# The first modulation on TensorE: weights stationary and columns out, half of the scales moved from VectorE and GpSimd

## The reference, cut to what matters

```python
c_act = jax.nn.silu(c)
cc_act = jax.nn.silu(c_ctx)
mod = (c_act @ ada_w[l] + ada_b[l])[:, None, :]
sh1, sc1, g1, sh2, sc2, g2 = jnp.split(mod, N_MOD, axis=-1)
h = modulate(x, sh1, sc1)          # h * (1.0 + scale) + shift
mod_c = cc_act @ ada_w[l] + ada_b[l]
csh1, csc1, ... = jnp.split(mod_c, N_MOD, axis=-1)
hc = modulate(x_ctx, csh1, csc1)
z = h @ w_in                       # the projections of layer 0
```

## Time and profile before

| | us |
|---|---|
| Median of 3 runs | 1854.79 |
| Lowest and highest | 1854.58, 1856.01 |
| Profiled execution | 1850.3 |
| Its span | 1848.4 |
| TensorE busy | 1786.0 (97%) |
| VectorE busy | 1272.5 (69%) |
| ScalarE busy | 891.5 (48%) |
| GpSimd busy | 1001.9 (54%) |

### The profile page before, as it was taken

How to read it: one execution, slowest core, us unless ns; L and a number is a source line. 1 busy time by engine, 2 the same in 40 slices (tenths; PEclk the granted TensorE clock), 3 DMA queues, 4 the chain that set the end, 5 groups by cost and what they waited for, 6 DMA issues and landing times.

```text
span 1848.4 us, 30888 instructions
## 1 busy us (share of the span) xinstructions
PE 1786.0 (97%) x10814; PEld 1535.7 (83%) x10814; DVE 1272.5 (69%) x2158; ACT 891.5 (48%) x1507; POOL 1001.9 (54%) x431
## 2 busy tenths in 40 slices
PE   5999899998999999999999999999999999999999
PEld 1847579997978887788878799999999988888887
DVE  6586667888548777424433369988999957777776
ACT  3033754445445454433353546665555554555553
POOL 4034146443775543775437778877776654444443
PEclk8999999999999999999999999999999999999999
DMA  8787247886665555543325455544544455555554
GB/s 324 260 302 252 87 145 239 281 278 214 209 204 182 182 193 165 178 159 114 103 92 171 159 173 182 182 163 163 166 160 149 149 184 193 193 192 194 193 193 169
DMA packets 95322, 346.00 MB, mean 187 GB/s; under 512 B 10544, under 2 KB 12032, under 8 KB 94592
## 3 DMA queue, kind: packets, MB, share of 16 engines
q1 hardware_dynamic: 78048, 283.67, 46.1%
q10 hardware_dynamic: 17184, 61.11, 9.5%
HBM read 343.66 MB, written 1.08 MB: 187 GB/s over the span
## 4 chain that ended last, share of the span: by engine, by line
PE 74%; DVE 12%; issue 6%; DMA 3%; POOL 3%; ACT 2%; DVEq 0%; ACTq 0%; POOLq 0%; SPq 0%
PE ps L626 26%; PE ps L561 19%; PE ps L573 6%; PE ps L579 3%; POOL ring_lo L506 3%; PE ps L696 2%; PE ps L782 2%; PE ps L545 2%; PE ps L849 2%; DMA ring<-stream 2%; PE ps L796 2%; PE ps L1014 1%; DVE arena L2812 1%; DVE ps L2809 1%; DMA cst<-consts 1%
## 5 line engine op out<-in xcount | busy, mean ns | idle before, releaser
L506 POOL TENSOR_TENSOR ring_lo<-ring,ring_hi 128x1024 fp32r<-128x1024 f32 x371 | 901.6, 2436 | 659.2 <-ACT ring_hi L500 657.6
L500 ACT ACTIVATE ring_hi<-ring 128x1024 fp32r<-128x1024 f32 x502 | 531.9, 1060 | 515.5 <-DMA ring<-stream 513.7
L561 PE MATMUL ps<-h_span,ring_hi 128*128 128x256 f32 x3168 | 416.2, 284 | 0.0
L561 PEld LDWEIGHTS ps<-h_span,ring_hi 128*128 128x128 f32 x3168 | 396.8, 192 | 5.5 <-issue 3.3
L626 PE MATMUL ps<-ring_hi,e_pair 128*128 128x512 f32 x1024 | 253.7, 389 | 0.8 <-DVE e_pair L2840 0.8
L2840 DVE TENSOR_TENSOR e_pair<-arena,e_pair 128x256 fp32r<-128x256 f32 x128 | 174.6, 1364 | 98.9 <-ACT e_pair L1850 98.2
L626 PEld LDWEIGHTS ps<-ring_hi,e_pair 128*128 128x128 f32 x1024 | 192.1, 188 | 41.0 <-issue 1.2
L561 PE MATMUL ps<-h_span,ring_lo 128*128 128x256 f32 x1584 | 222.4, 283 | 0.3 <-POOL ring_lo L506 0.2
L561 PEld LDWEIGHTS ps<-h_span,ring_lo 128*128 128x128 f32 x1584 | 204.3, 192 | 0.9 <-POOL ring_lo L506 0.9
L506 DVE TENSOR_TENSOR ring_lo<-ring,ring_hi 128x1024 fp32r<-128x1024 f32 x141 | 175.2, 1244 | 40.1 <-ACT ring_hi L500 39.9
L626 PE MATMUL ps<-ring_hi,arena_r 128*128 128x512 f32 x672 | 174.5, 392 | 2.2 <-ACT ring_hi L500 2.2
(11 more groups left out here) (301 smaller groups left out, 2305.4 us busy)
## 6 DMA issues: line engine op xcount, KB each, us to landing
ring<-stream SPq DMA_DIRECT2D x540, 512.0 KB, 3.3
arena<-aside_w ACTq DMA_DIRECT2D x49, 512.0 KB, 4.6
late<-aside_w ACTq DMA_DIRECT2D x21, 512.0 KB, 4.6
resid<-aside_w ACTq DMA_DIRECT2D x10, 512.0 KB, 5.8
arena<-scale_w ACTq DMA_DIRECT2D x8, 512.0 KB, 15.9
arena<-ln_rows ACTq DMA_DIRECT2D x8, 512.0 KB, 5.1
arena<-gate_cols ACTq DMA_DIRECT2D x2, 1024.0 KB, 4.9
arena<-decay ACTq DMA_DIRECT2D x1, 1536.0 KB, 6.8
```

Of the source, the lines that this page charges most:

```text
L500: act.activation(ring_hi[:, s, :], ring[:, s, :], ACT.Copy).then_inc(hi_ready, 1)
L506: eng.tensor_tensor(ring_lo[:, s, :], ring[:, s, :], ring_hi[:, s, :], ALU.subtract).then_inc(lo_ready[s], 1)
L561: m = pe.matmul(ps[:, bank, 0:T], w[:, kc * P:(kc + 1) * P], x[:, kc, :], start=begin, stop=w is w_lo and kc == KC - 1)
```

## The change

TensorE now makes twelve blocks: units 0 to 7 are the shifts and 8 to 11 the scale blocks 0 to 3. The weights are stationary, each unit in eight chunks of 128 x 128, and the two columns of `cact` are moving, so that the result comes out as columns in the bank (6, 7, then 3) and needs no copy and no turning. VectorE makes the scale blocks 4 to 7 as before; GpSimd and ScalarE make none. Chunks 4 to 7 of `sc1p` are released when shifts and VectorE's scales are there, chunks 0 to 3 after the third bank. Every chunk of `hcat` gives a semaphore step of its own, and the first projection takes them one by one, in the order 4, 5, 6, 7, 0, 1, 2, 3; the other front projections use the same order. The wait for the identity and the bias row stand after the first projection unit. ScalarE issues `x`, identity and small inputs before its activations of `c_all`, and the constants and `ctx` right after, before it waits for any result.

```diff
-EARLY_ADA = 8
-ASIDE = 2 * ADA_UNITS - 2 * EARLY_ADA
-SCALE_DVE = (0, 1, 2, 3, 4)
-SCALE_POOL = (5, 6, 7)
+EARLY_ADA = 12
+ASIDE = 2 * ADA_UNITS - 16
+SCALE_DVE = (4, 5, 6, 7)
...
-EARLY_BANKS = (4, 5)
+EARLY_BANKS = (6, 7, 3)
+FRONT_ORDER = (4, 5, 6, 7, 0, 1, 2, 3)
...
+            def k_tile(u, rhs, bank, at=0, done=True, first=False):
...
+                for kc in FRONT_ORDER:
+                    if first:
+                        pe.wait_ge(h_dve if kc < 4 else h_act, kc % 4 + 1)
...
-            def early_rows(g):
+            def early_tiles(g):
...
-                for k4 in range(4):
-                    w = unit(FIRST_UNIT["ada0"] + 4 * g + k4)
-                    for k2 in range(2):
-                        kc = 2 * k4 + k2
-                        m = pe.matmul(ps[0:2, b, :], cact[:, kc, :], w[:, k2 * 512:(k2 + 1) * 512],
+                for q in range(4):
+                    w = unit(FIRST_UNIT["ada0"] + 4 * g + q)
+                    for kc in range(KC):
+                        m = pe.matmul(ps[:, b, 2 * q:2 * q + 2], w[:, kc * P:(kc + 1) * P], cact[:, kc, :],
                                       start=kc == 0, stop=kc == KC - 1)
...
             for g in range(EARLY_ADA // 4):
-                early_rows(g)
-                if g == 0:
-                    pe.wait_ge(ident_in, 16)
-                else:
-                    early_columns(g - 1)
-            early_columns(EARLY_ADA // 4 - 1)
-            pe.wait_ge(inputs, 16 * 4)
-            bias_row()
+                early_tiles(g)
...
+                           done=tile_done(n) is not None, first=n == 0)
+                    if n == 0:
+                        pe.wait_ge(ident_in, 16)
+                        pe.wait_ge(inputs, 16 * 4)
+                        bias_row()
...
-            pe.wait_ge(h_dve, 1)
-            pe.wait_ge(h_act, 1)
             projections()
...
+            act.dma_start(h[:, :, :], x_t).then_inc(x_in, 16)
+            act.dma_start(cst[:, 0:P], consts[:, 0:P]).then_inc(ident_in, 16)
+            for dst, src in ((relb[0:32, :], rel_bias), (oneh[0:32, :], onehot), (dmask[0:8, :], dist_mask), (lamb, lam_in)):
+                act.dma_start(dst, src).then_inc(inputs, 16)
             for c, dst in enumerate((c_all, cc_all)):
                 act.wait_ge(c_in[c], 16)
                 act.activation(dst, dst, ACT.Silu).then_inc(c_all_ready, 1)
...
+            act.dma_start(cst[:, P:], consts[:, P:]).then_inc(consts_in, 16)
+            act.dma_start(z, ctx_t).then_inc(ctx_in, 16)
...
+            scale_column(0)
+            scale_column(1)
+            mod_columns(0, EARLY_BANKS[0], 0)
+            scale_column(2)
+            scale_column(3)
             settle()
+            step(dve.tensor_tensor(mod[0][:, SC1 + 4:SC1 + 8, :], mod[0][:, SC1 + 4:SC1 + 8, :],
+                                   param("ada_b0", SC1 + 4, 4).unsqueeze(2).broadcast_to([P, 4, 2]), ALU.add))
+            mod_columns(0, EARLY_BANKS[1], 4)
             settle()
+            for b in EARLY_BANKS[:2]:
+                dve.wait_ge(emptied[b], reads[b].now())
+            scales(4).then_inc(mod_cols, 1)
+            mod_columns(0, EARLY_BANKS[2], 8)
+            dve.wait_ge(emptied[EARLY_BANKS[2]], reads[EARLY_BANKS[2]].now())
+            step(scales(0))
+            settle()
```

More of the change, by code:

```diff
@@ L418, in build @@
         c_in = [sem(f"c_in{c}") for c in range(2)]
-        scale_w_in = [sem(f"scale_w_in{k}") for k in range(8)]
-        scale_product = sem("scale_product")
-        scale_sum = sem("scale_sum")
+        scale_w_in = [sem(f"scale_w_in{n}") for n in range(len(SCALE_DVE))]
         ident_in = sem("ident_in")
@@ L535, in wait_unit_lo @@
                 pe.wait_ge(lo_ready[u % RING], at_trip(i, TRIP // RING, SPLIT_IN_SLOT[u]))
-            def k_tile(u, rhs, bank, i=None, at=0, done=True):
-                w = unit(u, i)
+            def k_tile(u, rhs, bank, at=0, done=True, first=False):
+                w = unit(u)
                 if at == 0:
                     start_fill(bank)
-                for kc in range(KC):
+                for kc in FRONT_ORDER:
+                    if first:
+                        pe.wait_ge(h_dve if kc < 4 else h_act, kc % 4 + 1)
                     r = rhs(kc)
                     n = r.shape[-1]
-                    m = pe.matmul(ps[:, bank, at:at + n], w[:, kc * P:(kc + 1) * P], r, start=kc == 0, stop=kc == KC - 1)
-                    if kc == 0:
+                    m = pe.matmul(ps[:, bank, at:at + n], w[:, kc * P:(kc + 1) * P], r, start=kc == FRONT_ORDER[0],
+                                  stop=kc == FRONT_ORDER[-1])
+                    if kc == FRONT_ORDER[0]:
                         m.then_inc(units_begun, 1)
@@ L1340, in _ @@
                 act.dma_start(dst, all_rows(c_rows, c)).then_inc(c_in[c], 16)
-            for k in SCALE_LOADS[:5]:
-                scale_load(k)
+            for n in range(len(SCALE_DVE)):
+                act.dma_start(scale_in[:, n, :], scale_w[n]).then_inc(scale_w_in[n], 16)
             act.wait_ge(params_in, 16)
@@ L1365, in drain @@
                 act.activation(dst, ps[:, b, 0:n], func, **kw).then_inc(emptied[b], 1)
[L1367 to L1376, removed]
             n_var = Count()
@@ L1391, in _ @@
                 for kc in range(4, KC):
-                    m = act.activation(hcat[:, kc, (1 - c) * T:(2 - c) * T], src[:, kc, :], ACT.Identity,
-                                       scale=sc1p[:, kc, c:c + 1], bias=mod[0][:, SH1 + kc, c:c + 1])
-                m.then_inc(h_act, 1)
+                    act.activation(hcat[:, kc, (1 - c) * T:(2 - c) * T], src[:, kc, :], ACT.Identity,
+                                   scale=sc1p[:, kc, c:c + 1], bias=mod[0][:, SH1 + kc, c:c + 1]).then_inc(h_act, 1)
             def on_all(rows, k):
@@ L2881, in _ @@
             pool.wait_ge(c_all_ready, 2)
[L2882 to L2885, removed]
             for k in range(PAIRED):
@@ L3083, in _units @@
     return [
-        wide(a["ada_w"][0])[:EARLY_ADA], proj,
+        tiles(a["ada_w"][0])[:EARLY_ADA], proj,
         rows(np.concatenate([wo[:512], wo_b]))[list(MIX_ORDER)], *mlp(a["mlp_w1"][0], a["mlp_w2"][0]),
@@ L3099, in _aside @@
     columns = [w.T.reshape(ADA_UNITS, P, D) for w in a["ada_w"]]
-    return (np.ascontiguousarray(columns[0][SC1:SC1 + 8]),
+    return (np.ascontiguousarray(columns[0][[SC1 + k for k in SCALE_DVE]]),
             np.ascontiguousarray(np.stack([columns[l][at] for l, at in ASIDE_ORDER])))
```

72 lines of the change are left out of this document (19 added, 53 removed).

## The result

| | before | changed |
|---|---|---|
| Median of 22 runs each, us | 1850.97 | 1858.89 |
| Lowest and highest, us | 1845.56, 1858.01 | 1852.69, 1865.11 |
| Profiled execution and its span, us | 1850.3, 1848.4 | 1854.65, 1852.8 |
| First projection starts, us | 41.37 | 47.27 |

The changed kernel is slower: ratio 1.0032, interval 1.0021 to 1.0044, which is 3.9 to 8.1 us of 1851. The medians stand 7.9 us apart.

What follows compares the result with a forecast made beforehand. TensorE, busy 97% of the span, bounds the kernel, so the start of the projections counts: +7.4, bias row +0.8, clock +0.3 make +8.5 us (6.9 to 11.5), added to median 1854.8 for 1863.3 us; range 1857.5 to 1868.

Steps and rivals of the forecast that it cites:

- the gap at each unit: Early tiles on TensorE: waits for each unit's landing, 0.1 us for each of twelve, 1.2 us; bounds 0 and 3.0.
- the step from the front to the whole: Whole kernel: the front's +8.5 us added unchanged to the median 1854.8, giving 1863.3 us.
- The first rival: Early tiles: thin instructions earn full clock, weights' arrival bounds the front, 7.9 us faster, 1846.9 us; 12 in 100.
- The second: Early tiles: full clock for half the units gives 1858 us, for three quarters 1855; 4 in 100.
- 0.50 in the clock column from 20 us on: Front of the profile: granted clock shown as 0.50 until the projections, a sign that the forecast is right.
- The size of 0.213 us: Early tiles: each thin instruction at half clock, twice 0.107 us; 3.41 us a unit, 41.0 us for twelve.
- start of the first: Front of TensorE: the first early tile starts at 6.59 us, when the activated c is ready.
- projections begin, against before: End of the front: early tiles end at 48.8 us, so projections start 7.4 us later than at 41.4.
- bias row: After the first projection unit: formerly hidden, now on the path, adding 0.8 us.
- clock at the projections: Start of the projections: the clock's rise from half again costs time, 0.3 us more than before.
- the 48 to 50 that were to show me right: Start of the first projection: at 48 to 50 us with no idle time before it, a sign of being right.
- weights don't hold this up: Early tiles: TensorE asks for 154 GB/s, below the 206 that SP's queue gets when shared, so weights cost nothing.

Runs made afterwards that it cites:

- e1: Changed kernel with six wide products ahead of the first early tile; 1855.95 us in one run, kernel before 1854.45.
- e2: Changed kernel with six wide products first and two unread wider products after each early unit; 1855.90 us, ratio 1.0016 to the kernel before.
- e3: Changed kernel with its twelve TensorE units put back to wide rows, identity loaded early; 1850.96 us, ratio 0.9985 to the kernel before.
- e9: e5 with four more unread wide products in TensorE's pause before the projections; 1844.81 us, ratio 0.9957 to the kernel before.
- e5: Changed kernel with eight shift units as wide rows, all eight scale blocks on VectorE, identity early; 1846.98 us, ratio 0.9959 to the kernel before.
- e7: Kernel before, with the second group of wide rows not waiting for the identity; 1855.51 us, ratio 0.9990 to the kernel before.

## Why the prediction was right in its mechanism, and which steps failed

Direction and mechanism came as forecast: a slower kernel, because the thin instructions ran at half clock. The size did not. The front's sum had one term far too large, the gap at each unit (1.2 us for a measured 0.2), and the step from the front to the whole started from a median 3.8 us too high.

**What bounds.** Right: TensorE's main stream begins as the front ends, and takes the offset with it. In every row of the table above the offset at 100 us was still there at 300 us, within 1.7 us. Behind 300 us the scatter between executions, up to 8 us, is as large as the effect.

**The clock under thin tiles.** Right, and now shown: 192 at half clock by their spacing, e1 for the fall without a pause, e2 for the same instructions at 0.117 us among wide ones, e3 for the form undone. The first rival (full clock, 1846.9) is out. The second, full clock for a part, too: no thin instruction of the changed kernel ran fast. What I named as the sign of it, 0.50 in the clock column from 20 us on, did not show; that trace has no record there. The size of 0.213 us was partly luck. I doubled 0.107, which is 23 starts counted in 2.48 us; start to start the form stands 0.112 us apart at full clock (in e2 sixteen in 1.78 us, from 9.59 to 11.37). Twice that would have been 0.224 us, 43 us for the 192, where 41.1 were measured.

**The terms.** The front's sum was 8.5 us and the pair of traces shows 7.5:

| term | forecast, us | first pair of traces, us |
|---|---|---|
| thin instructions | 41.0 | 41.12 with all gaps |
| gap at each unit | 1.2 | in the above, 0.16 over 192 x 0.2133 |
| start of the first | 6.59 | 6.15 |
| projections begin, against before | +7.4 | +5.9 |
| bias row | +0.8 | +0.74 |
| clock at the projections | +0.3 | +0.9 |
| sum | +8.5 | +7.5 |

The mis-sized terms are the gaps and the start. I took the gap from projection units and scaled it by count: "0.1 x 12 = 1.2 us". In this trace there is next to none. ScalarE had one scale load less to issue ahead of `c`'s activation, which I did not count: 0.44 us. The first projection came at 47.3 us, outside the 48 to 50 that were to show me right. The clock term went the other way, 0.9 us for 0.3: 5.88 us for the first unit, where sixteen instructions at full clock take 3.4. That this made up for a third of the other misses is luck.

**From the front to the whole.** This step failed: "I add the same 8.5 to the median 1854.8". Both numbers in it were too high. The front of one trace of before, 41.37 us, was 0.7 us earlier than the second's 42.06, with 1.0 us at 100 us. The two pairs together give (7.5 + 7.2) / 2 - (0 + 1.0) / 2 = 6.9 us, the lower bound of the forecast's own sum. And the median of three runs stood 3.8 us over that of 22, with runs of the same kernel 12 us apart. The forecast time was 4.4 us above the measured 1858.9, and 3.8 of these are the base; 8.5 us on the later median would have been 1859.5. As a difference, 8.5 us is a little above the upper end of the measured 3.9 to 8.1 us.

**Beside the path.** Right: chunks 0 to 3 cost nothing, weights never were late, scales were done at 24.8 us, the tail is gone. But "weights don't hold this up" was true only of a slow TensorE, and the even split of the queues did not hold in e3.

Open: why the stages from 300 to 560 us differ between executions by several microseconds. The waits for split weights are where it shows; what starts them was not tried. Open too is why the clock falls at L1118 in some executions and not in others.

## What to carry to other kernels

Choosing which operand is stationary can choose the clock as well. Here a long run of products with two moving columns did not hold the clock and cost 0.213 us an instruction for 0.112, while the "wasteful" wide form of the same product raised the clock, and where no long pause followed, the stage behind it started at full clock (3.72 us for the first projection unit in e3 and e9, 5.9 in the changed kernel). When a chain of waits names one engine, see who finishes next to it before work is moved from the second to the first; here the cheap answer was to give VectorE all the scales without GpSimd beside it and leave TensorE alone (e5). e5 also loads the identity early and reorders the other loads; no run takes GpSimd away by itself. A difference of 0.3% at the front needs two traces of each kernel and some twenty runs: the same kernel's traces were 7 us apart for reasons behind the change.

## What the runs showed of the hardware

- VectorE's 1024-wide product with sum took 1.22 us alone and 3.35 us while GpSimd multiplied beside it (e7 and the kernel before against e5; in the kernel before also within one trace, 1.22 again once GpSimd was done). Sixteen of them alone were done at 32.2 us; ten, most of them beside GpSimd, at 37.7.
- Thirty-two thin instructions in a row don't always bring the clock down. In both traces of before it fell during L1118 (at 819.2 and 827.4 us); in the first trace of the changed kernel the same 32 stood 0.11 us apart to the end (32 in 3.49 us; PE timeline, 822 to 834 us) and the stretch behind kept 1.00. This is half of what the first trace "won back", the second place of L1118 the other half:

```profile
828.04 3.63 PE L1099 MATMUL ps<-cst,arena 128*128 128x2 f32 x32
831.53 1.10 PE L694 MATMUL ps<-arena,cst 128*128 128x512 f32 x2
```
- Two queues that both had loads under way did not always share evenly: 2.13 against 1.11 MB in 8 us of e3, where the forecast's stretch had 1.43 against 1.44.
